# Prompt attention of a hybrid layer step: values on halves of the array, scores three units ahead, the projection step in front of them

## What is computed

```python
def _mla_mixer(cq, ckv_raw, kpe_raw, pos, past, q_norm_g, w_qb, kv_norm_g, w_uk, w_uv):
    q = (_rmsnorm(cq, q_norm_g) @ w_qb).reshape(bsz, s, MLA_HEADS, MLA_NOPE + MLA_ROPE)
    q_lat = jnp.einsum('bshn,lhn->bshl', q[..., :MLA_NOPE], w_uk)
    q_pe = _rope(q[..., MLA_NOPE:], pos)
    ...
    o_lat = _mla_attend(q_lat, q_pe, pos, keys_ckv, keys_kpe, k_pos)   # causal softmax(scale * scores) @ latents
    o = jnp.einsum('bshl,lhv->bshv', o_lat, w_uv).reshape(bsz, s, MLA_WIDTH)
```

## Time and profile before

| | us |
|---|---|
| median of 3 runs | 3236.84 (3233.66 to 3237.91) |
| the profiled execution | 3235.72 |
| its span, first to last instruction | 3234.1 |
| PE busy in the span | 3056.2 (95%) |
| DVE busy | 1802.0 (56%) |
| ACT busy | 929.1 (29%) |
| mean granted TensorE clock | 0.958 of 2.4 GHz |

### The profile page before, as it was taken

One profiled execution on the slowest core, in us unless ns is written; L12 is line 12 of the kernel. 1 busy time (PEld: TensorE's weight loads), 2 busy tenths in 40 slices (PEclk: granted clock), 3 DMA queues, 4 the chain that ended last, 5 costly groups with the idle time before them and its releaser, 6 DMA issues. The chain is left out here.

```text
span 3234.1 us, 51727 instructions
## 1 busy us (share of the span) xinstructions
PE 3056.2 (95%) x21218; PEld 2736.5 (85%) x21218; DVE 1802.0 (56%) x3078; ACT 929.1 (29%) x1550; POOL 244.0 (8%) x280
## 2 busy tenths in 40 slices
PE   6987899998999999999989779989999999999998
PEld 5975577667999999999979546776699999999998
DVE  4856677553454545544566757865535545444554
ACT  4034444552311111111220444445423111111113
POOL 2000001540000000000020000025300000000000
PEclk8986999999999999999989779999999999999998
DMA  4112101762111111111031310047521111111201
GB/s 104 46 38 55 21 5 54 253 220 68 33 53 40 46 53 52 47 40 40 23 51 38 65 39 7 5 136 232 168 62 40 52 47 53 47 40 40 59 28 71
DMA packets 226587, 207.99 MB, mean 64 GB/s; under 512 B 50260, under 2 KB 195796, under 8 KB 226148
## 3 DMA queue, kind: packets, MB, share of 16 engines
q1 hardware_dynamic: 200744, 119.38, 13.6%
q0 software_dynamic: 25600, 85.11, 8.5%
HBM read 193.58 MB, written 11.05 MB: 63 GB/s over the span
## 5 line engine op out<-in xcount | busy, mean ns | idle before, releaser
L189 PE MATMUL ps<-streamH,upH 128*128 128x344 f32 x2112 | 449.2, 321 | 6.3 <-issue 5.0
L189 PE MATMUL ps<-streamH,upL 128*128 128x344 f32 x2112 | 447.4, 320 | 0.0
L189 PE MATMUL ps<-streamL,upH 128*128 128x344 f32 x2112 | 446.1, 320 | 0.0
L2266 ACT ACTIVATE upH<-hc 128x1024 fp32r<-128x1024 f32 x88 | 93.4, 1061 | 967.7 <-PE ps L189 967.7
L189 PEld LDWEIGHTS ps<-streamH,upH 128*128 128x128 f32 x2112 | 354.6, 188 | 8.7 <-issue 6.4
L189 PEld LDWEIGHTS ps<-streamH,upL 128*128 128x128 f32 x2112 | 356.1, 189 | 0.0
L189 PEld LDWEIGHTS ps<-streamL,upH 128*128 128x128 f32 x2112 | 352.8, 188 | 0.0
L2430 DVE TENSOR_TENSOR xT<-xT,ps 128x1032 f32<-128x1032 f32 x176 | 216.0, 1228 | 227.6 <-PE ps L189 227.6
L443 PE MATMUL ps<-inH,inW 128*128 128x344 f32 (+1 forms) x1248 | 234.1, 323 | 31.3 <-DVE inW L497 31.3
L2391 DVE TENSOR_TENSOR hc<-ps,rstd 128x1032 f32<-128x1032 f32 x44 | 54.2, 1232 | 370.7 <-PE ps L189 370.7
L443 PEld LDWEIGHTS ps<-inH,inW 128*128 128x128 f32 (+1 forms) x1248 | 198.9, 183 | 38.4 <-DVE inW L497 32.3
(11 more groups left out here) (472 smaller groups left out, 4899.4 us busy)
## 6 DMA issues: line engine op xcount, KB each, us to landing
hc<-in_w_ffn_in SPq DMA_DIRECT2D x88, 512.0 KB, 4.6
hc<-in_w_ffn_out SPq DMA_DIRECT2D x44, 512.0 KB, 3.7
big<-in_w_in SPq DMA_DIRECT2D x22, 512.0 KB, 3.9
stream_raw<-in_w_out SPq DMA_DIRECT2D x16, 512.0 KB, 4.0
big<-in_x_prompt SPq DMA_DIRECT2D x2, 2048.0 KB, 9.9
out_y_prompt<-big SPq DMA_DIRECT2D x8, 512.0 KB
scratch_y<-hc SPq DMA_DIRECT2D x16, 136.0 KB, 3.2
scratch_u<-wring SPq DMA_DIRECT2D x4, 516.0 KB, 3.1
```

The lines of the kernel that those rows point to most:

```text
L189: last = pe.matmul(self.ps[:, bank + n, 0:NCOL], w, x[:, n * NCOL:(n + 1) * NCOL], start=(k == 0 and i == 0), stop=(k == len(terms) - 1 an ...
L2266: act.activation(upH[u][:, :, :], raw[u], ACT.Copy).then_inc(g_wh[u], 1)
```

## The change

- **Order of units.** A pair's units now come in groups of four: for j = 0 to 3, head 0 with tiles 7 - j and j, then head 1 with tiles 7 - j and j. So an even unit has 8 to 5 key blocks (two banks of transposes) and an odd one 1 to 4 (one bank).
- **Values.** They run once for four units, after the fourth. The value columns are stationary (64 columns), the transposed exponentials stream (128 columns), and the two heads of the pair write partitions 0 to 63 and 64 to 127 of bank 7, one key block of each in turn. The result is already transposed, so `outputs` goes. The reciprocals are written 64 wide (`rden`), transposed by PE into the same bank, copied by ACT (`factors`), and DVE multiplies two tiles of results by them into `hc` (`output`).
- **Scores** go three units ahead: even units use banks 0 and 1 or 2 and 3, odd units bank 4. Transposes use banks 5 and 6, bank 7 is for steps and values.
- **Copies.** The first bank of an even unit is copied by DVE, all other banks by ACT.
- **Steps.** There are 10 (the keys in two cuts of 512 columns), in turns 0, 1, 2, 4, 5, 6, 8, 9, 10 and 12, and on PE a step stands between `transposes(u)` and `scores(u + 3)`. A step waits for the drain of the step before it, or, after a group's values, for their `output`; the values wait for the last step's drain.

```diff
-        order = [(v % 2, QT - 1 - v // 2 if v % 2 == 0 else v // 2) for v in range(NV)]
+        order = [(z, q) for j in range(4) for z in range(2) for q in (QT - 1 - j, j)]
...
-        STEPS = "DAAADDDAAAD"
+        copied_by = ["DA"[g] if u % 2 == 0 else "A" for u in range(NU) for g in range(banks_of[u])]
+        STEPS = "DAAADDDAAD"
         NS = len(STEPS)
-        step_at = {v: v - 2 for v in range(2, 1 + NS)}
-        step_at[NS + 2] = NS - 1
+        step_at = {v: j for j, v in enumerate((0, 1, 2, 4, 5, 6, 8, 9, 10, 12))}
+        VALUES_BANK = 7
...
+        def score_banks(u):
+            return ps[:, 2 * (u // 2 % 2):2 * (u // 2 % 2) + 2, :].rearrange("p b n -> p (b n)") if u % 2 == 0 else ps[:, 4, :]
...
-        kchunk = lambda c: slice(c * NCOL, min((c + 1) * NCOL, SEQ))
+        kchunk = lambda c: slice(c * 512, (c + 1) * 512)
...
                 def scores(u):
...
-                    if u >= 2:
+                    if u % 2 == 0 and u >= 4:
+                        pe.wait_ge(e_p, u - 3)
+                    if u % 2 == 1 and u >= 2:
                         pe.wait_ge(e_p, u - 1)
...
-                def values(u):
-                    p, z, q = units[u]
-                    pe.wait_ge(e_te, first_bank[u + 1])
-                    if u >= 1:
-                        pe.wait_ge(e_oe, u)
-                    h = 2 * p + z
-                    for kb in range(q + 1):
-                        last = pe.matmul(ps[:, 6, 0:V_DIM], pT[u % 2][:, kb * P:(kb + 1) * P], vt[:, kb, h * V_DIM:(h + 1) * V_DIM],
-                                         start=(kb == 0), stop=(kb == q))
+                def values(i):
+                    p, j = i // 4, i % 4
+                    drained(pe, values_of[i] - 1)
+                    pe.wait_ge(e_r, 4 * i + 4)
+                    for w in range(2):
+                        pe.transpose(ps[:, VALUES_BANK, (2 * w + 1) * P:(2 * w + 2) * P], rden[w], ident)
+                    for at in (first_bank[4 * i + 4] - 1, first_bank[4 * i + 2], first_bank[4 * i + 3] - 1):
+                        copied(pe, at)
+                    for w, q in ((1, QT - 1 - j), (0, j)):
+                        for kb in range(q + 1):
+                            for z in range(2):
+                                h = 2 * p + z
+                                last = pe.matmul(ps[64 * z:64 * z + 64, VALUES_BANK, 2 * w * P:(2 * w + 1) * P], vt[:, kb, h * V_DIM:(h + 1) * V_DIM],
+                                                 pT[w][z][:, kb * P:(kb + 1) * P], start=(kb == 0), stop=(kb == q))
                     last.then_inc(e_o, 1)
...
-                scores(0)
-                scores(1)
+                for u in range(3):
+                    scores(u)
...
                     transposes(u)
-                    if u + 2 < NU:
-                        scores(u + 2)
-                    if u >= 1:
-                        values(u - 1)
-                    if v == 1 and p:
-                        outputs(p - 1, 1)
                     if v in step_at and p + 1 < PAIRS:
                         step(p + 1, step_at[v])
-                    if v == 14:
-                        outputs(p, 0)
+                    if u + 3 < NU:
+                        scores(u + 3)
+                    if v % 4 == 3:
+                        values(u // 4)
...
                 for u in range(NU):
                     p, v = u // NV, u % NV
-                    if u >= 1:
-                        output(u - 1)
+                    if u and u % 4 == 0:
+                        factors(u // 4 - 1)
+                    copies(u)
                     if u + 2 < NU:
                         exponentials(u + 2)
...
                 for u in range(NU):
                     p, v = u // NV, u % NV
-                    copies(u)
+                    if u and u % 4 == 0:
+                        output(u // 4 - 1)
+                    if u % 2 == 0:
+                        copies(u)
                     reciprocals(u)
-                    if u + 2 < NU:
-                        maxima(u + 2)
+                    if u + 3 < NU:
+                        maxima(u + 3)
                     if v in step_at and p + 1 < PAIRS and STEPS[step_at[v]] == "D":
                         drain(p + 1, step_at[v])
```

More of the change, by code:

```diff
@@ L1253, in mla_prompt @@
         e_te = self.sem("e_te")
+        e_ta = self.sem("e_ta")
+        e_rt = self.sem("e_rt")
         e_o = self.sem("e_o")
@@ L1273, in mla_prompt @@
         cosq, sinq = take(TOKENS)[0:64], take(TOKENS)[0:64]
-        otok = [take(D_MODEL).rearrange("p (q c) -> p q c", q=QT) for _ in range(2)]
+        small_pT = [take(512) for _ in range(2)]
+        rden = [take(P) for _ in range(2)]
+        rT = take(2 * P)
         wukT = W(0, 256).rearrange("p (z c) -> p z c", z=2)
@@ L1419, in step @@
                     last.then_inc(e_ax, 1)
[L1421 to L1427, removed]
                 def scores(u):
@@ L1439, in scores @@
                         w = min(512, n - c)
-                        last = pe.matmul(ps[:, 2 * (u % 2) + c // 512, 0:w], query[p % 2][z][0:KQ, q * P:(q + 1) * P],
+                        last = pe.matmul(score_banks(u)[:, c:c + w], query[p % 2][z][0:KQ, q * P:(q + 1) * P],
                                          keys[p % 2][z][0:KQ, c:c + w], start=True, stop=True)
@@ L1476, in _ @@
                         pe.wait_ge((e_va, e_vd)[t % 2], t // 2)
-                    pe.matmul(ps[:, 4 + t % 2, :], T(11)[:, t * P:(t + 1) * P], wuv, start=True, stop=True).then_inc(e_vm, 1)
+                    pe.matmul(ps[:, 5 + t % 2, :], T(11)[:, t * P:(t + 1) * P], wuv, start=True, stop=True).then_inc(e_vm, 1)
                 pe.wait_ge(e_va, QT // 2)
@@ L1520, in drain @@
                     k, w = step_of[p, j], p % 2
-                    bank = 2 + k % 6 if p == 0 else 7
-                    act.wait_ge(e_ax, k + 1)
+                    bank = 2 + k % 6 if p == 0 else VALUES_BANK
+                    act.wait_ge(e_ax, NS * p + j + 1)
                     for z in range(2):
@@ L1526, in drain @@
                     last.then_inc(e_xa, 1)
[L1528 to L1533, removed]
                 def exponentials(u):
@@ L1556, in _ @@
                     act.wait_ge(e_vm, t + 1)
-                    act.activation(vt[:, t, :], ps[:, 4, :], ACT.Copy).then_inc(e_va, 1)
+                    act.activation(vt[:, t, :], ps[:, 5, :], ACT.Copy).then_inc(e_va, 1)
                     if t == 0:
@@ L1591, in drain @@
                     k, w = step_of[p, j], p % 2
-                    bank = 2 + k % 6 if p == 0 else 7
-                    dve.wait_ge(e_ax, k + 1)
+                    bank = 2 + k % 6 if p == 0 else VALUES_BANK
+                    dve.wait_ge(e_ax, NS * p + j + 1)
                     if j == 0:
@@ L1634, in reciprocals @@
+                    if u >= 4:
+                        dve.wait_ge(e_p, u - 3)
+                    TS(slot(0, u), slot(2, u), -MLA_SCALE, None, ALU.mult).then_inc(e_nb, 1)
                 def reciprocals(u):
+                    p, z, q = units[u]
                     dve.wait_ge(e_p, u + 1)
-                    if u >= 2:
-                        dve.wait_ge(e_oe, u - 1)
-                    dve.reciprocal(st[:, 4 + u % 2:5 + u % 2], st[:, 2 + u % 2:3 + u % 2]).then_inc(e_r, 1)
+                    if u // 4:
+                        dve.wait_ge(e_o, u // 4)
@@ L1640, in copies @@
+                    dve.reciprocal(rden[1 - u % 2][:, 64 * z:64 * z + 64], slot(1, u).to_broadcast([P, 64])).then_inc(e_r, 1)
                 def copies(u):
-                    p, z, q = units[u]
-                    for g in range(banks_of[u]):
-                        at = first_bank[u] + g
-                        w = (min(4 * g + 4, q + 1) - 4 * g) * P
-                        dve.wait_ge(e_t, at + 1)
-                        if u >= 2:
-                            dve.wait_ge(e_o, u - 1)
-                        dve.tensor_copy(pT[u % 2][:, 4 * g * P:4 * g * P + w], ps[:, 4 + at % 2, 0:w]).then_inc(e_te, 1)
@@ L1649, in _, with output @@
-                for j in (0, 4, 5, 6, 10):
+                    at = first_bank[u]
+                    dve.wait_ge(e_t, at + 1)
+                    if u // 4:
+                        dve.wait_ge(e_o, u // 4)
+                    dve.tensor_copy(pT[1][units[u][1]][:, 0:512], ps[:, 5 + at % 2, :]).then_inc(e_te, 1)
+                def output(i):
+                    p, j = i // 4, i % 4
+                    dve.wait_ge(e_rt, i + 1)
+                    blocks = hc[:, 2 + p, 0:SEQ].rearrange("p (a c) -> p a c", c=P)
+                    TT(blocks[:, j:QT - j:QT - 1 - 2 * j, :], ps[:, VALUES_BANK, :].rearrange("p (w x c) -> p w x c", w=2, x=2)[:, :, 0, :],
+                       rT.rearrange("p (w c) -> p w c", w=2), ALU.mult).then_inc(e_oe, 1)
@@ L1650, in _ @@
+                for j in (0, 4, 5, 6, 9):
                     drain(0, j)
-                maxima(0)
-                maxima(1)
+                for u in range(3):
```

(3 more changed lines are left out.)

89 lines of the change are left out of this document (45 added, 44 removed).

## The result

The changed kernel takes **3287.05 us** (median of 4 runs, 3281.88 to 3288.91) against 3237.38 (4 runs, 3233.66 to 3242.12): a ratio of **1.015, 95% interval 1.0131 to 1.0169**. It is slower, by 49.7 us; the forecast was 3268 with a range of 3238 to 3305. The profiled execution after took 3281.88 us with a span of 3280.2, 46.1 over the span of before.

A forecast was written before the change was run, and what follows sets the result against it. PE was taken as the bound (50.65 of 51.40 us busy in a pair with steps), with new waits outweighing its saving. 3235.7 + 21 (two layers) + 12 (clock) = 3268.7, forecast 3268 us, range 3238 to 3305.

The forecast's parts named there:

- The round of step, scores, maxima and drain: In a pair with steps, time from a DVE-drained step to the next: 5.47 us against 3.3 of PE's own work.
- The blocks: Four turns each of a pair with steps: 12.6, 16.05, 16.35, 11.85, together 56.85 us against 51.4 before.
- The clock: PE's waits over 1 us lower the granted clock: 2 us a pair with steps, +12 in all.
- two dips a pair: Stretches at a granted clock near 0.50 after PE waits, two a pair with steps, each up to 1.7 us of work.
- later waits absorb about half: Of the two dips' cost in a pair with steps, later waits hide about half, leaving 2 us a pair.
- The wide reciprocal: DVE's reciprocal 64 wide instead of one (0.156 us): between nothing and 0.1 us more, taken as 0.07.
- Ahead of the loop: A third score and its maximum push back DVE's first copy of the values' matrix: +0.6 us (0 to 1.7).
- the last pair of each layer: Pair without steps, nothing drained: 37.4 us against 45.2, so -7.8.
- the signs that were named: Pairs with steps 55 to 60 us, last under 40, PE 70 to 80% busy, waits naming DVE, value matmuls every 0.054 us.
- The values: PE's turn of values for four units: 2.35 us with two transposes; PE saves 7.0 us of work a pair.
- Rival 2: Value matmuls' halves don't overlap: +1.9 us for each of 32 turns, 3330 us; chance 0.06.
- Rivals 1 and 3: Rival 1: PE's saving counts in full, 3180 us, chance 0.09; rival 3: waits a quarter smaller, clock steady, 3236, chance 0.06.

The follow-up runs named there:

- Experiments 1 and 2: Changed kernel with PE's step behind scores(u+3): 3233.78 us; changed kernel with DVE's drain ahead of maxima(u+3), step still before scores: 3251.86 us.
- the kernel without dips: Changed kernel, step behind scores, reciprocal one wide, rotated sums and samples' copies moved, DVE's copy before maxima in turn 13: 3200.11 us.
- experiment 4: Changed kernel with the values' loops exchanged, all key blocks of head 0, then all of head 1: 3320.03 us (one run).
- experiment 6: Changed kernel with DVE's reciprocal taken one column wide and spread to 64 columns by a copy: 3276.95 us, ratio 1.0119.

## Why the prediction was right, and where it was short

The direction, the mechanism and the range held; the time came 18 us above the sum of 3268.7. Of these, 13 show between the two profiled executions (spans 46.1 apart, forecast 33). The other 5 are that the execution profiled after was the fastest of its four, 5.2 under their median; its mean granted clock was 0.956, that of the others 0.951 to 0.955.

- **The order.** The round of step, scores, maxima and drain was put at 5.47 us against 3.3 of PE's own work, and took 5.29. Experiments 1 and 2 show that it is what lengthens a pair with steps.
- **The blocks.** Forecast 12.6, 16.05, 16.35, 11.85; measured 12.84, 16.23, 19.60 (16.82 without its dips), 11.99. The sums are nearer than their parts: in the first block the forecast had 10.5 of work and 2.1 of waits, the row has 11.44 and 1.40, so work put too low and waits put too high made up for each other. In the whole pair 14.1 us of waits were forecast and the four rows leave 11.46 idle, so the nearness is in part luck. Without dips a pair takes 57.90 us where 56.85 was forecast, and the first pair of a layer 57.75 where 56.5 was: 6.7 us over the six pairs, the largest part of the 13.
- **The clock** was put too low as well. Two us a pair with steps were forecast, 12 in all. In both layers the blocks are longer than their dipless 16.24, 16.83 and 11.99 by 15.8 us together, 3.8 more than forecast: third blocks of 20.00, 19.60, 19.00, 19.82, 18.28 and 18.23, one second block of 17.76, and 0.36 in a fourth. The rows that are not shown above:

```profile
391.46:411.46 20.00, 15.20 (x77) 9.77 (x78) 12.93 (x31) 7.60 (x17) 0.00 (x0) 0.83 0.00 0
513.13:532.13 19.00, 14.09 (x78) 9.36 (x76) 12.94 (x31) 7.60 (x17) 0.00 (x0) 0.86 0.00 1
2005.64:2025.46 19.82, 15.27 (x79) 10.04 (x77) 12.94 (x31) 7.51 (x17) 0.00 (x0) 0.83 0.00 0
2050.29:2068.05 17.76, 14.27 (x83) 9.37 (x81) 10.33 (x23) 6.16 (x15) 0.00 (x0) 0.90 0.00 1
2068.05:2086.33 18.28, 13.36 (x79) 8.80 (x77) 12.93 (x31) 7.60 (x17) 0.00 (x0) 0.92 0.00 1
2127.39:2145.62 18.23, 13.31 (x78) 8.75 (x77) 12.94 (x31) 7.60 (x17) 0.00 (x0) 0.91 0.00 0
```

  About two dips a pair was the right count (ten in the six pairs, one of them twice as costly) and 1.7 us each the right price; the step that failed is "later waits absorb about half". Of the 18.1 us of work lost, 15.8 were paid.
- **The wide reciprocal** was taken at 0.07 us over the narrow one, with 0.1 as the upper bound, and is 0.39 over it (545 against 156 ns). The bound was wrong: the trace of before had no row for it, and the width was counted like that of a copy.
- **Small terms.** Ahead of the loop +1.5 us where 0.6 was forecast (0 to 1.7); the last pair of each layer 38.8 where 37.4 was (2.8 together); the first pair's first block 12.76, with hardly less wait than the others. Of the signs that were named, pairs of 55 to 60 us and a busy share of 70 to 80% were just passed (60.4 to 60.9 us, 0.80 to 0.81); the others came (value matmuls every 0.059 us where 0.054 was named).
- **The values.** 2.46 us with the two transposes (433.77 to 436.23) for a forecast of 2.35; PE's work in a pair fell from 50.65 to 44.22 in the kernel without dips, by 6.4 where 7.0 was forecast. Rival 2 is out, by 0.059 us a matmul and by experiment 4. The rule of the Trainium skill ("TensorE: Matmul & The Clock Gate", Part 3) that weight loads overlap matmuls in flight only where row groups differ, from which the prediction took that nothing would overlap, doesn't fit these halves of columns, whose matmuls start 0.059 us apart.
- **Rivals 1 and 3.** Neither came. The faster one had its condition right: 3200 us is what comes where drains and most copies are over before PE asks, and 3180 had the halves' gain whole.

Not settled is which waits bring a dip. In the changed kernel's profiled execution the same waits come back in all six pairs with steps: a dip begins within 1 us of the end of the wait of 1.80 in all six, of the wait of 1.84 in three, and of the wait of 1.81 in one; none follows that of 1.46. In the second pair of the second layer the wait of 1.81 has one behind it (a step of 2.31 us for 1.42) and that of 1.84 has none, the other way round than in the pair shown above:

```profile
2059.02 2.31 PE L1419 MATMUL ps<-big,wring 128*128 128x344 f32 x4 [1.81 <-DVEq L1605]
2073.30 1.12 PE L1422 MATMUL ps<-big,wring 128*128 128x512 f32 x2 [1.84 <-DVEq L1605]
```

Filling two waits took the dips of the third block away; a rule for the rest isn't shown.

## What to carry to other kernels

Before a step is moved in front of work that feeds another engine, write down what stands ahead of its drain on that engine's queue: if the drain is behind an operation that needs the moved-past work, the step's buffer comes round only once per round trip, and the engine that was the bound begins to wait. An engine at 0.98 busy that is given 13% less work doesn't get 13% faster: the next queue must be put in order first, block by block, and a wait taken from one block can come back whole in the next. Price an operation that is made wider from a row of that operation, not from a copy's.

## What the runs showed of the hardware that was not expected

- DVE's reciprocal goes by width far more steeply than a copy: 128x64 takes 545 ns and 128x1 157, about 6.2 ns for each further column, while a copy of 128x64 from one column takes 199 ns and one of 128x512 684.
- Matmuls on two halves of 64 columns, in turn, start 0.059 us apart for 128 columns of stream; one after the other they cost 0.097 (3.48 us for 36), and at the border of two groups they still overlap.
- Waits of PE under 2 us can be followed by a dip to a granted clock of 0.50 that takes 1.7 us of its work, and waits of the same length in the same execution are not (1.84 us: three of six). Moving 0.2 us on DVE changed the places of the dips (experiment 6: none in the second pair's third block, one in its fourth).
